# A two-block transformer kernel on one core: IN by quarters of K, modulation by 512 features and partly summed on VectorE, the second norm from columns

## The chip, the core and the metric

The kernel runs on one core of a Trainium2 chip. The metric is device time in microseconds of one execution (us).

## What is computed

Two transformer blocks follow each other on `x` (256 tokens, 2048 features, float32). The change touches the first alone:

```python
mod = silu(c) @ w_ada + b_ada                     # 2048 -> 6 * 2048
sh1, sc1, gt1, sh2, sc2, gt2 = split(mod, 6)
h = rmsnorm(x, g_norm_mix) * (1 + sc1) + sh1
proj = h @ w_in                                   # 2048 -> 3072: xr, gr, xp
xr = causal_dwconv(xr); hr = rg_lru(xr)
y = concat([hr * gelu(gr), pool_mixer(xp)]) @ w_out
x = x + gt1 * y
h = rmsnorm(x, g_norm_ffn) * (1 + sc2) + sh2
x = rmsnorm(x + gt2 * ((silu(h @ w_ffn_gate) * (h @ w_ffn_up)) @ w_ffn_down))
```

The second block (projection, retention, windowless block attention, merge, convolved FFN) is computed by code that the change leaves alone but for semaphore counts.

## The kernel before

Activations lie feature-major: 16 blocks of 128 features by 256 tokens. Each product runs in **slabs** of 256 output features and **chunks** of 512 rows of K (`KT` = 4 blocks of 128). A chunk's weights are 512 KB. Chunks are numbered through the program as G: IN has slabs 0 to 11 (G 0 to 47), OUT 12 to 19 (G 48 to 79), FFN1 starts at slab 20 (G 80) with gate and up slabs in turn.

Float32 values are multiplied as a high and a low part of type fp32r. Per chunk SP loads `raw` (a ring of 8), ACT copies the high part into `split` (a ring of 4, `convert` L793), DVE writes the low part (`convert` L1118), and PE multiplies each block of 128x128 twice (L512 and L514): high weights by the high and low activations side by side, 512 columns, and low weights by the high activations, 256 columns:

```python
pe.matmul(ps[:, s, b, :], split[:, slot, k, 0, ...], acts[:, k0 + k, :, :], ...)    # 512 columns
mm = pe.matmul(ps[:, s, b, 0:T], split[:, slot, k, 1, ...], acts[:, k0 + k, 0, :], ...)  # 256
```

A slab's product is then evicted: ACT copies the half with the low activations (`copy_low` L801, line L806), DVE adds the other (`evacuate` L1124, L1132). PE waits for the eviction of the slab before last.

**The modulation** is 12 parts of 1024 features; a part is 8 pieces of 1 MB (256 rows of K by 1024 columns). `multiply_ada` (L523, matmuls at L539) multiplies one piece by `c_act`, four products side by side in the array's columns; after the eighth ACT copies the row (`copy_row` L826, line L830), `turn_ada` (L543, matmuls at L547) turns it into a column and `finish_ada` (L1155, line L1158) adds the bias. Two parts (the scale and the shift of features 0 to 1023) come ahead of IN. The others **ride**: `RIDE_AT` (L95) names the chunk behind which a piece is multiplied, one a chunk in G 0 to 15, then four in five chunks. The pieces' loads stand in SP's one queue ahead of the weights of chunk G + 8, each waiting for its slot in a ring of 4, later of 2. Part 11 is stored in another order and read with a step of 8 (L537). Four pieces (`FILLERS`, L96) are multiplied while PE waits for the second norm.

**IN** runs its first eight slabs in two halves of K (`half_slab` L612): sixteen chunks over features 0 to 1023 of h, whose partial sums DVE keeps in `xr_pad` and `pool_x`, then sixteen over the rest, whose h is made at the border (L858 on ACT, L1202 on DVE). Convolution, gates, windows and recurrence follow in helpers called between chunks (`first_mid`, L924 on ACT and L1383 on DVE).

**The second norm** lies between OUT and FFN1: DVE sums the squares (L1173), PE spreads the sum over all partitions with a matrix of ones (`sum_squares` L559, L566 and L567), DVE, ACT and DVE form 1/rms over 256 columns (L1177, L854, L1188), then each block is scaled (L1197), shifted and rounded (L858), and its low part taken (L1202). FFN1's first slab waits for four blocks per chunk.

## Time and profile before

| | us |
|---|---|
| median of 3 runs (lowest, highest) | 2656.75 (2651.25, 2659.0) |
| the profiled execution, its own time | 2656.45 |
| its span | 2654.7 |
| TensorE busy | 2581.5 (97%) |
| VectorE busy | 1715.6 (65%) |
| ScalarE busy | 1183.7 (45%) |

Busy time is what an engine spent in instructions. The span runs from the first to the last instruction; the execution's own time lies 1.75 us above it. The mean granted TensorE clock is 0.986.

### The profile page before, as it was taken

The page shows a single profiled execution, that of the slowest core. Times are in us where ns is not written, and L with a number is a line of the kernel's source. Part 1 is how long each engine was busy: PE and PEld are TensorE (multiplying, and loading weights), DVE is VectorE, ACT ScalarE, POOL GpSimd, SP SyncE. Part 2 cuts the span into 40 slices and gives each one's busy share as a digit, 9 for nine tenths or more (in the row PEclk, how much of TensorE's full clock was granted, in tenths as well). Part 3 has the DMA queues.
Part 4 walks back from the last instruction along what each step waited for, and adds up shares of the span by engine and source line. Part 5 has one row for each costly group of instructions (what it writes and reads, how often), then busy time and mean ns, then how long its engine had stood idle before and what let it go on. Part 6 is the DMA issues. An engine that isn't in the chain of part 4 may idle for free.

```text
span 2654.7 us, 40107 instructions
## 1 busy us (share of the span) xinstructions
PE 2581.5 (97%) x14708; PEld 2140.2 (81%) x14708; DVE 1715.6 (65%) x2235; ACT 1183.7 (45%) x1441; POOL 9.9 (0%) x37
## 2 busy tenths in 40 slices
PE   4999998999999999999999999999999999999997
PEld 0667665788888888888888888888888888888886
DVE  2568445455555555577677565577788758875886
ACT  1345334344444444463444454455544444444443
POOL 1000000000000000000000000000000000000000
PEclk8999998999999999999999999999999999999998
DMA  9978988655555555565555555555555555565553
GB/s 374 400 272 328 348 328 296 211 190 190 190 190 189 191 189 189 164 190 179 178 172 172 167 163 188 189 184 189 174 190 189 183 185 183 185 192 181 189 171 114
DMA packets 155797, 553.91 MB, mean 209 GB/s; under 512 B 15648, under 2 KB 19744, under 8 KB 155696
## 3 DMA queue, kind: packets, MB, share of 16 engines
q1 hardware_dynamic: 154848, 549.84, 61.3%
q0 software_dynamic: 848, 2.69, 0.3%
q8 instruction: 67, 1.10, 0.2%
q14 instruction: 34, 0.28, 0.0%
HBM read 550.38 MB, written 2.10 MB: 208 GB/s over the span
## 4 chain that ended last, share of the span: by engine, by line
PE 92%; DMA 3%; DVE 2%; ACT 1%; issue 1%; SPq 0%; DVEq 0%; ACTq 0%
PE ps L512 55%; PE ps L514 28%; PE pm L539 3%; DMA ride<-in_w_ada 3%; PE ps L507 2%; PE ps L509 1%; DVE split L1121 1%; ACT split L799 0%; PE pm L547 0%; PE pm L684 0%; PE pm L608 0%; DVE x_t L1224 0%; DVE h_s L1423 0%; DVE val L1132 0%; ACT sq_gf L845 0%
## 5 line engine op out<-in xcount | busy, mean ns | idle before, releaser
L1121 DVE TENSOR_TENSOR split<-raw,split 128x1024 fp32r<-128x1024 f32 (+1 forms) x864 | 1032.5, 1203 | 808.2 <-ACT split L799 803.6
L799 ACT ACTIVATE split<-raw 128x1024 fp32r<-128x1024 f32 (+1 forms) x864 | 897.6, 1043 | 1211.5 <-PE ps L514 1154.1
L512 PE MATMUL ps<-h_s,split 128*128 128x512 f32 x3904 | 1383.5, 399 | 11.4 <-DVE split L1121 6.4
L514 PE MATMUL ps<-h_s,split 128*128 128x256 f32 x3904 | 1091.4, 280 | 0.0
L512 PEld LDWEIGHTS ps<-h_s,split 128*128 128x128 f32 x3904 | 735.0, 188 | 231.8 <-issue 54.5
L512 PE MATMUL ps<-mid_s,split 128*128 128x512 f32 x2368 | 833.3, 397 | 0.7 <-DVE split L1121 0.7
L514 PEld LDWEIGHTS ps<-h_s,split 128*128 128x128 f32 x3904 | 738.1, 189 | 0.5
L514 PE MATMUL ps<-mid_s,split 128*128 128x256 f32 x2368 | 661.7, 279 | 0.0
L512 PEld LDWEIGHTS ps<-mid_s,split 128*128 128x128 f32 x2368 | 444.3, 188 | 124.6 <-issue 17.3
L514 PEld LDWEIGHTS ps<-mid_s,split 128*128 128x128 f32 x2368 | 446.5, 189 | 0.0
L539 PE MATMUL pm<-ride,c_act 128*1 128x512 f32 x768 | 119.9, 703 | 39.0 <-DMA ride<-in_w_ada 39.0
L806 ACT ACTIVATE low<-ps 128x512 f32<-128x512 f32 x232 | 134.6, 580 | 4.4 <-PE ps L514 4.4
L507 PE MATMUL ps<-split,h_s 128*128 128x512 f32 x256 | 91.2, 401 | 0.0
L1132 DVE TENSOR_TENSOR val<-ps,low 128x512 f32<-128x512 f32 x128 | 87.4, 683 | 3.8 <-ACT low L806 3.7
L1503 DVE SCALAR_TENSOR_TENSOR conv_o<-up_pad,par,conv_o 128x256 f32<-128x256 f32 x176 | 77.5, 482 | 11.4 <-DVE conv_o L1501 5.6
L539 PEld LDWEIGHTS pm<-ride,c_act 128*1 128x1 f32 x768 | 10.6, 81 | 84.6 <-DMA ride<-in_w_ada 46.7
L509 PE MATMUL ps<-split,h_s 128*128 128x256 f32 x256 | 71.8, 280 | 0.0
L1134 DVE TENSOR_TENSOR low<-ps,low 128x512 f32<-128x512 f32 x88 | 60.1, 683 | 0.2
L507 PEld LDWEIGHTS ps<-split,h_s 128*128 128x128 f32 x256 | 48.1, 188 | 13.3 <-issue 1.7
L509 PEld LDWEIGHTS ps<-split,h_s 128*128 128x128 f32 x256 | 48.3, 189 | 0.0
L512 PE MATMUL ps<-o_r,split 128*128 128x512 f32 x128 | 45.5, 398 | 0.0
L512 PE MATMUL ps<-o_m,split 128*128 128x512 f32 x128 | 44.9, 393 | 0.0
(225 smaller groups left out, 1030.7 us busy)
## 6 DMA issues: line engine op xcount, KB each, us to landing
raw<-in_w_in SPq DMA_DIRECT2D x224, 512.0 KB, 3.4
ride<-in_w_ada SPq DMA_DIRECT2D x88, 1024.0 KB, 7.8
raw<-in_w_ffn_down SPq DMA_DIRECT2D x128, 512.0 KB, 3.9
raw<-in_w_ffn_gate SPq DMA_DIRECT2D x88, 512.0 KB, 3.5
raw<-in_w_ffn_up SPq DMA_DIRECT2D x88, 512.0 KB, 3.8
raw<-in_w_ffn_a SPq DMA_DIRECT2D x88, 512.0 KB, 3.9
raw<-in_w_ffn_b SPq DMA_DIRECT2D x88, 512.0 KB, 4.4
raw<-in_w_out SPq DMA_DIRECT2D x64, 512.0 KB, 5.1
```

Source lines behind the costliest of these rows:

```text
L507: pe.matmul(ps[:, s, b, :], acts[:, k0 + k, 0, b * P:(b + 1) * P], split[:, slot, k, :, :].rearrange("p h n -> p (h n)"), start=start, sto ...
L509: mm = pe.matmul(ps[:, s, b, 0:SLAB], acts[:, k0 + k, 1, b * P:(b + 1) * P], split[:, slot, k, 0, :], start=False, stop=stop)
L512: pe.matmul(ps[:, s, b, :], split[:, slot, k, 0, b * P:(b + 1) * P], acts[:, k0 + k, :, :].rearrange("p h t -> p (h t)"), start=start, sto ...
L514: mm = pe.matmul(ps[:, s, b, 0:T], split[:, slot, k, 1, b * P:(b + 1) * P], acts[:, k0 + k, 0, :], start=False, stop=stop)
L539: mm = pe.matmul(pm[2 + n % 2][g:g + 1, :], c_act[:, k:k + 1], moving, start=(i == 0), stop=(i == PIECES - 1))
L799: act.activation(split[:, c, 0:kt, 0, :], raw[:, CHUNKS * s + c, 0:kt, :], ACT.Copy).then_inc(hi_ready, 1)
L806: act.activation(low[:, s, :, :], ps[:, s, :, T:2 * T], ACT.Copy).then_inc(low_copied, 1)
L1121: dve.tensor_tensor(split[:, c, 0:kt, 1, :], raw[:, CHUNKS * s + c, 0:kt, :], split[:, c, 0:kt, 0, :].bitcast(F32), ALU.subtract).then_inc ...
L1132: ins = dve.tensor_tensor(dst, ps[:, s, :, 0:T], both, ALU.add)
L1134: own(dve.tensor_tensor(both, ps[:, s, :, 0:T], both, ALU.add))
L1503: ins = dve.scalar_tensor_tensor(out=dst, in0=src, scalar=w, in1=dst, op0=ALU.mult, op1=ALU.add)
```

## The change

1. **Groups of 512 features.** Scale and shift of the first norm (parts 0 to 3) become eight groups (`UNITS`) of four 1 MB pieces, each 512 rows of K by 512 columns. Only the first two groups stand ahead of IN; the others ride in G 0 to 20, eight pieces in five of each eight chunks. Five further parts ride from G 24, one piece a chunk in eight of nine chunks.
2. **IN in quarters of K.** The first eight slabs run in four passes of eight chunks (`one_chunk`). Each block is multiplied by three matmuls of 256 columns into one sum. ACT copies the sums of the first pass, DVE adds those of the others to them; ACT's `copy_low` isn't needed there. The h blocks of the next pass are made in chunks 3 to 6 of the pass before. The helpers between chunks get new places (`GATES_AT`, `WINDOWS_AT`, `POOL_AT`).
3. **Three parts are summed on DVE**: part 7 in OUT (G 60 to 75), parts 10 and 11 in FFN1 (G 88 to 119). A load of 128 rows (512 KB) is multiplied by `c_act` and added to a 128x1024 sum, and PE turns the sum with eight small matmuls (`turn_sums`). The fillers go.
4. **The second norm from columns.** PE takes the sum of squares as one column per 128 tokens, 1/rms is formed on 128x2, put on a diagonal and spread by two matmuls. ACT loads the table of the square root ahead of OUT. FFN1's first gate and up slabs take turns chunk by chunk, and the gate's wait for each block of h (`first_pair`).

The core of the diff:

```diff
-ADA_ORDER = (2, 0, 3, 1, 4, 5, 8, 6, 9, 7, 10, 11)
+LATE_PARTS = (4, 5, 8, 6, 9, 7, 10, 11)
+UNITS, UNIT_PIECES = 2 * CHUNKS, 4
+TENSOR_PARTS = 5
+OUT_ADDS = 1 * DB
+OUT_ADD_RING, FFN_ADD_RING = 6, 4
...
 def _rides():
-    at = list(range(HALF_CHUNKS))
-    at += [HALF_CHUNKS + r + r // 4 for r in range(6 * PIECES)]
-    at += [CHUNKS * 20 - 1] * (FILL_BEFORE + FILL_AFTER)
-    at += [CHUNKS * 20 + 2 + 2 * r for r in range(2 * PIECES - FILL_BEFORE - FILL_AFTER)]
+    at = [PASS_SLABS * p + c for p in range(CHUNKS - 1) for c in (0, 0, 1, 1, 2, 3, 3, 4)]
+    at += [PASSES - PASS_SLABS + r + r // 8 for r in range(TENSOR_PARTS * PIECES)]
     return at
...
+ADD_AT = [CHUNKS * 15 + j for j in range(OUT_ADDS)] + [CHUNKS * 22 + j for j in range(2 * DB)]
+GATES_AT = (26, 28, 30, 32)
+WINDOWS_AT = (32, 33, 37, 42)
+POOL_AT = (34, 36, 40, 44)
...
+        def load_add(j):
+            where, slot, _ = add_slot(j)
+            if j == 0:
+                sp.wait_ge(chunk_used, CHUNKS * S_OUT)
+            elif j == OUT_ADDS:
+                sp.wait_ge(ada_multiplied, UNITS * UNIT_PIECES + TENSOR_PARTS * PIECES)
+            if OUT_ADD_RING <= j < OUT_ADDS:
+                sp.wait_ge(ada_added, j - OUT_ADD_RING + 1)
+            elif j >= OUT_ADDS + FFN_ADD_RING:
+                sp.wait_ge(ada_added, j - FFN_ADD_RING + 1)
...
+            sp.dma_start(where, src).then_inc(add_loaded[slot], 16)
...
+        def turn_sums(g):
+
+            pe.wait_ge(ada_added, DB * (g - ADD_GROUPS + 1))
+            pe.wait_ge(mod_ready, g - 1)
+            sums = ada_sums(g)
+            for j in range(8):
+                block = sums[:, j * P:(j + 1) * P] if late_part(g) < ADA_FIRST else \
+                    sums.rearrange("q (p j) -> q j p", j=8)[:, j, :]
+                mm = pe.matmul(pm[2 + g % 2][:, j:j + 1], block, ones[:, 0:1], start=True, stop=True)
             mm.then_inc(ada_turned, 1)
...
+        def one_chunk(G):
+
+            c, q = divmod(G, PASS_SLABS)
+            if G >= 2:
+                pe.wait_ge(evacuated, G - 1)
+            if q == 0:
+                pe.wait_ge(h_ready, KT * (c + 1))
+            pe.wait_ge(lo_ready, G + 1)
+            for k in range(KT):
+                for b in range(2):
+                    weights = split[:, G % RING, k, :, b * P:(b + 1) * P]
+                    out, acts = ps[:, G % 2, b, 0:T], h_s[:, c * KT + k, :, :]
+                    pe.matmul(out, weights[:, 0, :], acts[:, 0, :], start=(k == 0), stop=False)
+                    pe.matmul(out, weights[:, 0, :], acts[:, 1, :], start=False, stop=False)
+                    mm = pe.matmul(out, weights[:, 1, :], acts[:, 0, :], start=False, stop=(k == KT - 1))
+            mm.then_inc(chunk_used, 1)
+            ride_along(G)
...
-        sum_squares(1)
-        for piece in FILLERS:
-            multiply_ada(piece)
-
+
+
+        pe.wait_ge(ssq_added, OUT_SLABS * 2)
+        for b in range(2):
+            for k in range(2):
+                mm = pe.matmul(pm[1][:, b:b + 1], ssq[:, k, b * P:(b + 1) * P], ones[:, 0:1], start=(k == 0), stop=(k == 1))
+        mm.then_inc(ssq_summed, 1)
+        pe.wait_ge(diag_ready, 1)
+        for b in range(2):
+            mm = pe.matmul(pm[1][:, T + b * P:T + (b + 1) * P], ones[:, :], diag[:, b, :], start=True, stop=True)
+        mm.then_inc(rstd_spread, 1)
+
+
+        def first_pair(gu):
+
+            for i in range(2 * CHUNKS):
+                G, s, c = CHUNKS * gu + i, i % 2, i // 2
+                if c == 0:
+                    pe.wait_ge(evacuated, evac_count_of(gu + s) - 1)
+                multiply(G, G % RING, s, h_s, c * KT, KT, c == 0, c == CHUNKS - 1,
+                         ready=DB + c * KT if s == 0 else None)
...
+            if c > 0:
+                dve.wait_ge(chunk_used, G + 1)
+                if G == PASS_SLABS:
+                    dve.wait_ge(evacuated, PASS_SLABS)
+                dve.tensor_tensor(pass_sum(q), ps[:, G % 2, :, 0:T], pass_sum(q), ALU.add).then_inc(evacuated, 1)
...
+            if c < CHUNKS - 1 and q == 6:
+                for b in range(first, first + KT):
+                    norm_low(0, 0, b)
```

**PE, the opening of IN.** Rows with `ride` and `ride_88` (or `ride_89`) are pieces of the modulation, `sel,row` the turns, `ps` the products of IN. Before, from the sum of squares on:

```order
L566 MATMUL pm<-ssq,ones 128x256
L567 MATMUL pm<-ssq,ones 128x256
L539 MATMUL pm<-ride,c_act 1x512 x4
L539 MATMUL pm<-ride_88,c_act 1x512 x8
L547 MATMUL pm<-sel,row 128x2 x4
L539 MATMUL pm<-ride,c_act 1x512 x8
L539 MATMUL pm<-ride_88,c_act 1x512 x8
L539 MATMUL pm<-ride,c_act 1x512 x8
L539 MATMUL pm<-ride_88,c_act 1x512 x8
L547 MATMUL pm<-sel,row 128x2 x4
L512 MATMUL ps<-h_s,split 128x512
L514 MATMUL ps<-h_s,split 128x256
```

Now, from the same instruction:

```order
L650 MATMUL pm<-ssq,ones 128x256
L651 MATMUL pm<-ssq,ones 128x256
L599 MATMUL pm<-ride_89,c_act 1x512 x4
L616 MATMUL pm<-sel,row 128x1 x4
L599 MATMUL pm<-ride,c_act 1x512 x8
L599 MATMUL pm<-ride_89,c_act 1x512 x8
L616 MATMUL pm<-sel,row 128x1 x4
L708 MATMUL ps<-h_s,split 128x256
L709 MATMUL ps<-h_s,split 128x256
L710 MATMUL ps<-h_s,split 128x256
```

IN's first matmul stands behind 32 matmuls of the modulation and not 64, and comes in threes.

**SP, from the first weights of IN.** Before:

```order
L384 DMA raw<-in_w_in 128x1024 x8
L396 DMA ride<-in_w_ada 128x2x1024
L384 DMA raw<-in_w_in 128x1024
L396 DMA ride<-in_w_ada 128x2x1024
L384 DMA raw<-in_w_in 128x1024
L396 DMA ride_88<-in_w_ada 128x2x1024
L384 DMA raw<-in_w_in 128x1024
```

The queue now:

```order
L422 DMA raw<-in_w_in 128x1024 x8
L437 DMA ride<-in_w_ada 128x4x512 x2
L422 DMA raw<-in_w_in 128x1024
L437 DMA ride_89<-in_w_ada 128x4x512 x2
L422 DMA raw<-in_w_in 128x1024
L437 DMA ride<-in_w_ada 128x4x512
L422 DMA raw<-in_w_in 128x1024
L437 DMA ride<-in_w_ada 128x4x512
L437 DMA ride_89<-in_w_ada 128x4x512
L422 DMA raw<-in_w_in 128x1024
L437 DMA ride_89<-in_w_ada 128x4x512
L422 DMA raw<-in_w_in 128x1024 x4
```

One piece and one chunk of weights took turns here; now the eight pieces of a group pair stand in front of five of eight chunks.

**SP, the loads for chunks 60 and on**, in OUT. `raw` is a chunk of weights, `add_out` a load for a sum on DVE. Before, in OUT:

```order
L384 DMA raw<-in_w_out 128x1024
L396 DMA ride<-in_w_ada 128x2x1024
L384 DMA raw<-in_w_out 128x1024
L396 DMA ride<-in_w_ada 128x2x1024
L384 DMA raw<-in_w_out 128x1024 x2
```

Now:

```order
L441 DMA ride<-in_w_ada 128x2x1024
L456 DMA add_out<-in_w_ada 128x1024
L422 DMA raw<-in_w_out 128x1024
L441 DMA ride<-in_w_ada 128x2x1024
L456 DMA add_out<-in_w_ada 128x1024
L422 DMA raw<-in_w_out 128x1024
```

The loads of the sums stand between the pieces and the weights, for eight chunks with both.

## Rows read from the trace of the kernel before

**Rows 1.** The page, part 1: busy us, share of the span, instructions.

```profile
PE 2581.5 (97%) x14708; PEld 2140.2 (81%) x14708; DVE 1715.6 (65%) x2235; ACT 1183.7 (45%) x1441; POOL 9.9 (0%) x37
```

**Rows 2.** The chain of waits in order of time: start, us, what.

```profile
59.19 1.93 PE pm L539 x8
...
69.72 0.77 PE ps L512
...
78.04 0.97 PE pm L539 x8
...
109.80 0.97 PE pm L539 x8
```

**Rows 3.** The instruction timeline of PE, the eighth piece: start, us, line, operation.

```profile
37.28 1.89 PE L539 MATMUL pm<-ride,c_act 128*1 128x512 f32 x8 [0.91 <-DMA ride<-in_w_ada]
```

**Rows 4.** Table of windows, 70 to 134 us; DMA packets of 3:13 and 19:31.

```profile
70.00:134.00 64.00, 64.00 (x383) 41.97 (x383) 31.12 (x39) 23.89 (x29) 0.00 (x0) 0.98 1.01 403
DMA packets 2489, 3.63 MB, mean 363 GB/s; under 512 B 52, under 2 KB 2100, under 8 KB 2489
DMA packets 1254, 4.86 MB, mean 405 GB/s; under 512 B 67, under 2 KB 67, under 8 KB 1254
```

**Rows 5.** Timeline, the end of one chunk with its ride, and the next.

```profile
130.00 0.40 PE L512 MATMUL ps<-h_s,split 128*128 128x512 f32 x1
...
130.23 0.28 PE L514 MATMUL ps<-h_s,split 128*128 128x256 f32 x1
...
130.44 1.04 PE L539 MATMUL pm<-ride,c_act 128*1 128x512 f32 x8
...
131.41 0.50 PE L512 MATMUL ps<-h_s,split 128*128 128x512 f32 x1
131.52 0.19 PEld L514 LDWEIGHTS ps<-h_s,split 128*128 128x128 f32 x1
```

**Rows 6.** Timeline, weight loads of a turn.

```profile
390.11 0.98 PEld L547 LDWEIGHTS pm<-sel,row 128*128 128x128 f32 x8
```

**Rows 7.** Timeline, the border between the halves of K.

```profile
134.44 1.04 PE L539 MATMUL pm<-ride,c_act 128*1 128x512 f32 x8
...
137.82 0.69 DVE L1132 TENSOR_TENSOR pool_x<-ps,low 128x512 f32<-128x512 f32 x1
...
138.54 3.26 DVE L1202 SCALAR_TENSOR_TENSOR h_s<-xc,mod,h_s 128x256 fp32r<-128x256 f32 x8
...
140.32 0.76 PE L512 MATMUL ps<-h_s,split 128*128 128x512 f32 x1 [3.06 <-issue]
...
145.06 1.04 PE L539 MATMUL pm<-ride,c_act 128*1 128x512 f32 x8
```

**Rows 8.** Timeline, a piece of part 11 in FFN1, and the next chunk.

```profile
452.49 2.01 PE L539 MATMUL pm<-ride,c_act 128*1 128x512 f32 x8
454.43 0.50 PE L512 MATMUL ps<-h_s,split 128*128 128x512 f32 x1
```

**Rows 9.** Timeline, the second norm and FFN1's first chunks.

```profile
404.98 1.22 PE L566 MATMUL pm<-ssq,ones 128*128 128x256 f32 x2 [3.54 <-DVE ssq L1173]
...
409.86 0.88 DVE L1197 SCALAR_TENSOR_TENSOR val<-x_t,gain,rstd 128x256 f32<-128x256 f32 x2
...
422.67 0.48 DVE L1202 SCALAR_TENSOR_TENSOR h_s<-val,mod,h_s 128x256 fp32r<-128x256 f32 x1 [0.18 <-ACT h_s L858]
...
419.77 0.80 PE L512 MATMUL ps<-h_s,split 128*128 128x512 f32 x1
...
430.28 1.04 PE L539 MATMUL pm<-ride,c_act 128*1 128x512 f32 x8
```

**Rows 10.** Waits of PE, 206 to 400 us: us, times, longest.

```profile
PE pm L539 <- DMA ride<-in_w_ada: 2.0, 4, 0.8
```

**Rows 11.** Windows, 514 to 600 us (PE, PEld, DVE, ACT); a DVE group of the page by shapes.

```profile
514.00:600.00 86.00, 86.00 (x498) 75.23 (x497) 49.65 (x50) 38.38 (x43) 0.00 (x0) 1.00 0.58 189
L1327 DVE SCALAR_TENSOR_TENSOR lru_t<-a_sq,lru_t 128x1024 f32<-128x1024 f32 x2 | 2.5, 1226 | 0.1
```

More of the change, by code:

```diff
@@ L499, in slab, with multiply @@
                     after(c)
-        def multiply(G, slot, s, acts, k0, kt, first, last, tok=False):
+        def multiply(G, slot, s, acts, k0, kt, first, last, tok=False, ready=None):
             pe.wait_ge(lo_ready, G + 1)
             for k in range(kt):
+                if ready is not None:
+                    pe.wait_ge(h_ready, ready + k + 1)
                 start, stop = first and k == 0, last and k == kt - 1
@@ L960, in pool_high @@
             ins.then_inc(pool_hi, 1)
[L962 to L966 removed]
+        for G in range(PASSES):
+            ahead = G + RING
+            convert(ahead // (2 * CHUNKS), ahead // CHUNKS % 2, ahead % CHUNKS)
+            if G < PASS_SLABS:
+                act.wait_ge(chunk_used, G + 1)
+                act.activation(pass_sum(G), ps[:, G % 2, :, 0:T], ACT.Copy).then_inc(evacuated, 1)
+            first_mid(G)
+            if G % PASS_SLABS == 6 and G < PASSES - PASS_SLABS:
+                first = KT * (G // PASS_SLABS + 1)
+                act.wait_ge(mod_ready, first // 2 + 2)
+                for b in range(first, first + KT):
+                    norm_block(0, 0, b)
+        for q in range(PASS_SLABS, IN_SLABS):
+            turn(q // 2, q % 2, mid=lambda c: first_mid(CHUNKS * q + c))
         gelu(3)
         y_high(3)
+        act.activation(s_inv[:, :], inv_n[:, 0:2], ACT.Sqrt)
         for q in range(OUT_SLABS):
@@ new lines, in finish_rides @@
+        def finish_rides(G):
+            for g, at in LAST_RIDE.items():
+                if at + 1 == G:
+                    finish_ada(g)
+            for j, at in enumerate(ADD_AT):
+                if at == G:
+                    k, sums = j % DB, ada_sums(ADD_GROUPS + j // DB)
+                    piece, slot, times = add_slot(j)
+                    dve.wait_ge(add_loaded[slot], 16 * times)
+                    if k == 0:
+                        dve.tensor_scalar(sums, piece, c_act[:, k:k + 1], None, ALU.mult).then_inc(ada_added, 1)
+                    else:
+                        dve.wait_ge(ada_added, j)
+                        dve.scalar_tensor_tensor(out=sums, in0=piece, scalar=c_act[:, k:k + 1], in1=sums,
+                                                 op0=ALU.mult, op1=ALU.add).then_inc(ada_added, 1)
+            for g, at in LAST_ADD.items():
+                if at + 3 == G:
+                    a = late_part(g) * 8
+                    dve.wait_ge(ada_turned, g + 1)
+                    dve.tensor_tensor(mod[:, a:a + 8], pm[2 + g % 2][:, 0:8], col("b_ada", a, 8), ALU.add).then_inc(mod_ready, 1)
@@ L1416, in _ @@
+        for q in range(PASS_SLABS, IN_SLABS):
+            turn(q // 2, q % 2, val[:, q % 2, :, :], mid=lambda c: first_mid(CHUNKS * q + c))
         gated(3)
```

532 lines of the change are left out of this document (272 added, 260 removed).

## The prediction

> **What bounds the kernel now.** I read the page first: TensorE is busy for 97% of the span [rows 1]. So time is won where it idles or does work that can go elsewhere; the modulation and its waits lie ahead of about 510 us. The chain of waits, read in order of time, gives the opening: sixteen 1 MB modulation pieces land one by one, the last is multiplied at 59.19, and the first matmul of IN starts at 69.72 [rows 2]. The eighth piece was multiplied at 37.28 [rows 3]. The table of windows says what holds this stage: the DMA engines are full (403 GB/s in the first 16 chunks) while TensorE never pauses [rows 4]. The instruction timeline gives prices: a chunk with its ride goes from 130.44 to 134.44; over the eight from 78.04 to 109.80 in the chain it is 3.97 us [rows 2, 5]. A chunk alone is 8 pairs of matmuls, 498 matmuls in 86.00 us, so 0.345 a pair and 2.77 a chunk [rows 11]. A ride thus costs 1.19, of which 0.97 is its own (130.44 to 131.41 [rows 5]) and 0.22 the change-over. Two holes are left: the second half of K, no matmul of IN from 135.4 to 140.32 [rows 7], and the second norm, where FFN1 starts at 419.77 [rows 9].
>
> The sum is made against the profiled execution's 2656.45 us (span 2654.7), 0.3 below the median of the runs. A difference under 0.3% (8 us) can't be told from none.
>
> **The change, part by part.**
>
> *Start: -20.7.* Only two groups of four pieces precede IN. They use the same ring, so the eighth comes where it did, and the path behind the last piece keeps its length (59.19 to 69.72 is 10.53: turn, gain, four blocks of norm, first conversion). That moves the start by 59.19 - 37.28 = 21.9. But the pieces now come in rows of 2 KB. Of the trace's packets, 2489 of 1.46 KB on average took 10 us of 16 engines, 64 ns each, and 1254 of 3.9 KB took 12 us, 153 ns each [rows 4]. Between them 2 KB costs about 86 ns, so a piece (512 packets, 16 engines) takes 2.7 us, not 2.55, and eight pieces 1.2 us more. IN starts near 49.
>
> By the Trainium skill ("DMA: Bandwidth & Descriptors", the overview table) anything from 512 B up runs at line rate, so this 1.2 us and the first pass's share of as much would not exist, and the time would be 2617. The rows above differ, and I go by them.
>
> *First pass: +2.2.* By SP's order, shown with the change, eight raw chunks (4.2 MB, 10.2 us at 410 GB/s) go ahead of the third group's pieces. With piece 8 of the run landing near 51.4 and a piece or chunk behind it every 2.7 or 1.27 us, the rides at chunks 1 and 3 wait about 1 us each for their second piece, and the pass ends near 86. From then on a pass moves 12.6 MB in 32 us and TensorE needs 34, so no wait is left.
>
> *Borders of K: -1.2.* The border before costs 4.9 idle (135.41 to 140.32) and 1.8 at the low clock (that chunk took 4.74, not 2.97), 6.7 in all [rows 7]. Now there are three. At each, ACT and DVE first convert, DVE adds the pass sum (0.69), and then four low parts at 0.41 (eight took 3.26 [rows 7]): ready 4.9 behind chunk 6's end, where chunk 7 covers 2.8. That is 2.1 twice, and 1.3 in the first pass (its sum is on ACT): 5.5.
>
> *Rides: -21.7.* Before, 96 pieces: 16 in the opening, 6 in the norm's hole, 74 on the path at 1.19, and part 11's eight, read with a stride, take 0.97 more each (452.49 to 454.43 [rows 8]): 88.1 + 7.8 = 95.9. Now 64: three passes with eight pieces in five chunks (8 x 0.97 + 5 x 0.22 = 8.9) and forty singles, 26.6 + 47.6 = 74.2.
>
> *Turns: +9.4.* A turn is 8 records in 0.98, 0.93 on the path [rows 6]. Nine become eleven (8.3 to 10.2), and three sums of 16 records come in, 1.9 each, the last by eight-strided weights, which I double as the pieces' stride does [rows 8]: 7.5. Left alone it would be 1.9 less.
>
> *Three matmuls for two: -2.4.* In eight slabs a pair of 512 and 256 columns becomes three of 256. The 512 starts 0.23 before the 256, the next comes 0.12 behind it [rows 5]. Three at 0.112 are 0.336 for 0.345, times 256. The doubt is the weight load, which lasts 0.19 and now has only short matmuls above it. The row of turns answers: eight loads of 128x128 back to back in 0.98, one in 0.11 [rows 6]. If loads didn't overlap it would be 3 x 0.19, +56 in all: the upper bound, far from that row.
>
> By the Trainium skill ("TensorE: Matmul & The Clock Gate", Back-to-back issue gap) a matmul costs N/2.4 + 2.5 ns, so a third one would only add a floor, +0.6. The trace's 512-column start distance of 0.23 is longer than that, which is where my gain comes from.
>
> *Second norm: -8.0.* Ahead of it little changes: TensorE's sums over 256 columns (from 404.98), and the statistics and reciprocal over 256 columns until the first scaled block at 409.86 [rows 9] become eight records of one column (about 1.9 at the low clock), small instructions and one spread, from which I get 409.2. The gain is behind: the first pair takes h block by block. Blocks come every 0.79 (409.86 to 422.67 for 16), TensorE starts at the first, near 411.3, does chunks 80 to 83 (11.1, and 2.3 for the low clock, as 419.77 to 430.28 is 10.5 for 3 x 2.77 and the change-over) and is through at 424.4, just as ACT and DVE deliver chunk 84. Before it would be there at 432.9, rides apart. Half a us goes back at chunk 88, which waits for the gate's eviction one chunk earlier.
>
> *Sums in OUT and FFN1: +5.* 48 DVE instructions of 128x1024, 1.23 each [rows 11]. In FFN1 a pair of slabs has 22.2 us; DVE is busy 49.65 of 86, 12.9 a pair, and eight sums make it 22.7. That is as much as there is, but conversions run four chunks ahead (6 us in hand), so four such pairs cost nothing; without this cover they cost 2 to 6. What does cost is OUT: chunks 60 to 67 have ride, sum and weights, 2.1 MB or 5.1 us at 410 GB/s, against 3.97. Eight times 1.14 is 9.1, the upper bound; zero is the lower, if queued loads run ahead. Chunk 59 has no ride, so the queue begins some 4 us ahead: I take 5. Rides waited 2.0 in four places before [rows 10], and I leave that as it is. SP's other loads keep eight chunks of lead. The weights' reordering in FFN1's first pair, the longer unrolled part and the removed evictions on ACT lie under TensorE's work: 0.
>
> Sum: -20.7 + 2.2 - 1.2 - 21.7 + 9.4 - 2.4 - 8.0 + 5 = -37.4, so **2619**.
>
> **The rivals.**
> 1. *DVE or ACT binds*, in slabs 8 to 11 (decays in two adjacent chunks, four windows, both multipliers, with about 2 us in hand by my count) and in FFN1. For: 22.7 against 22.2. Against: DVE is busy for 65% over the span, and the ring of four is deep. Price 4 and 6: 2629.
> 2. *DMA binds more than I take*: OUT's full 9.1, the passes another 4, and a wait behind every eighth ride: 2629. For: 403 GB/s in the stage at issue [rows 4]. Against: the 16-chunk stage there ran on without a pause.
> 3. *A third matmul gains nothing*: if each short one starts 0.12 behind the last, as the 512 does behind the 256, three take 0.36 against 0.345, +3.8 and not -2.4: 2625. For: 0.12 is read at 0.01 [rows 5]. Against: the turns' 0.11 [rows 6]. The floor of the Trainium skill's page on TensorE points the same way.
> 4. *The early start is swallowed*: the change doesn't do what it says, since the bytes of IN bind and TensorE waits out what it won, 2640. Against: until pass 3 ends some 67 MB move, 166 us at 403 GB/s, and TensorE isn't there before about 190.
> 5. *Slower: weight loads bind.* In IN's eight slabs no long matmul covers two loads. It decides once a load's distance passes 0.19 us, and three at 0.19 make 0.56: 2619 + 2.4 + 56 = 2677. Rows 6 speak against it.
>
> **How the numbers follow.** Forecast 0.55, rival 1 0.14, rival 2 0.12, rival 3 0.06, rival 4 0.06, rival 5 0.04, the rest 0.03 for something unforeseen. The low end takes OUT's 5 and the first pass's 2.2 as nothing, an unhurt strided turn and a border or two that close: 2608. The high end adds rival 1's 10, two borders with the low clock (1.8 each) and 4 of OUT's bound: 2637. Outside are rivals 4 and 5 and a tail. Faster by over 0.3% is every case but rival 5 and part of the rest: 0.94, same 0.01, slower 0.05.
>
> **What would show it.** First IN matmul near 49 (start); rides waiting for DMA in chunks 0 to 4 alone (first pass); idle of 1 to 2 us ahead of chunks 8, 16 and 24 at the full clock (borders); a chunk of 24 matmuls in 2.7 us (three for two; 4.5 would be rival 5); FFN1's first matmul near the first block of h and some 13 us later the fifth chunk (norm); waits on ride pieces in chunks 60 to 67 of 5 in sum (OUT), and none on split in FFN1. The prediction is wrong if TensorE waits for split, for the pass sums or for `mod` anywhere ahead of 480 us, or if the time behind FFN1's second group differs from before.

## The result

| | us |
|---|---|
| before, median of 6 runs (lowest, highest) | 2657.34 (2651.25, 2659.45) |
| the change, median of 6 runs (lowest, highest) | 2635.09 (2630.65, 2646.09) |
| ratio of the two, 95% interval | 0.9926 [0.991, 0.9941] |
| predicted | 2619.0 (2608 to 2637) |
| the change's profiled execution (span) | 2646.09 (2644.3) |

The change gains about 20 us (0.74%, between 16 and 24 us by the interval). The direction is right and the median lies in the range, but the forecast was 37: about half of it came. The profiled execution is the slowest of its six.

### The profile page after: what moved, and what is told of

The parts are those of the page before. It is cut to its first block, busy times and chain, and to the rows that moved or that the text cites. A ratio compares the mean times of both kernels' runs of the same rounds, so it can differ in the third digit from the quotient of the medians.

```text
span 2644.3 us, 40425 instructions
## 1 busy us (share of the span) xinstructions
PE 2567.1 (97%) x14836; PEld 2170.0 (82%) x14836; DVE 1771.2 (67%) x2291; ACT 1182.5 (45%) x1436; POOL 9.9 (0%) x37
## 4 chain that ended last, share of the span: by engine, by line
PE 90%; DMA 4%; DVE 3%; ACT 1%; issue 1%; SPq 0%; DVEq 0%; ACTq 0%
PE ps L576 53%; PE ps L578 27%; DMA ride<-in_w_ada 4%; PE ps L571 2%; PE ps L573 1%; PE ps L708 1%; PE pm L599 1%; DVE split L1225 1%; PE ps L710 1%; PE ps L709 1%; PE pm L606 1%; ACT split L907 1%; PE pm L792 0%; DVE xc L1406 0%; DVE val L1318 0%
## 5 line engine op out<-in xcount | busy, mean ns | idle before, releaser
L576 PE MATMUL ps<-h_s,split 128*128 128x512 f32 x3648 | 1295.7, 400 | 4.1 <-DVE h_s L1323 1.7
L578 PE MATMUL ps<-h_s,split 128*128 128x256 f32 x3648 | 1023.9, 281 | 0.0
L576 PEld LDWEIGHTS ps<-h_s,split 128*128 128x128 f32 x3648 | 687.2, 188 | 186.4 <-issue 16.3
L578 PEld LDWEIGHTS ps<-h_s,split 128*128 128x128 f32 x3648 | 690.6, 189 | 0.4
L913 ACT ACTIVATE low<-ps 128x512 f32<-128x512 f32 x216 | 125.2, 579 | 4.4 <-PE ps L578 4.4
L708 PE MATMUL ps<-h_s,split 128*128 128x256 f32 x256 | 76.6, 299 | 11.2 <-DVE split L1225 6.1
L709 PE MATMUL ps<-h_s,split 128*128 128x256 f32 x256 | 73.5, 287 | 0.0
L710 PE MATMUL ps<-h_s,split 128*128 128x256 f32 x256 | 73.4, 287 | 0.0
L708 PEld LDWEIGHTS ps<-h_s,split 128*128 128x128 f32 x256 | 50.0, 195 | 25.7 <-issue 24.8
L599 PE MATMUL pm<-ride,c_act 128*1 128x512 f32 x256 | 37.2, 681 | 26.0 <-DMA ride<-in_w_ada 26.0
L571 PEld LDWEIGHTS ps<-split,h_s 128*128 128x128 f32 x256 | 48.1, 188 | 13.3 <-issue 1.7
```

The lines of the kernel that those rows point to most:

```text
L571: pe.matmul(ps[:, s, b, :], acts[:, k0 + k, 0, b * P:(b + 1) * P], split[:, slot, k, :, :].rearrange("p h n -> p (h n)"), start=start, sto ...
L576: pe.matmul(ps[:, s, b, :], split[:, slot, k, 0, b * P:(b + 1) * P], acts[:, k0 + k, :, :].rearrange("p h t -> p (h t)"), start=start, sto ...
L578: mm = pe.matmul(ps[:, s, b, 0:T], split[:, slot, k, 1, b * P:(b + 1) * P], acts[:, k0 + k, 0, :], start=False, stop=stop)
L708: pe.matmul(out, weights[:, 0, :], acts[:, 0, :], start=(k == 0), stop=False)
L709: pe.matmul(out, weights[:, 0, :], acts[:, 1, :], start=False, stop=False)
L710: mm = pe.matmul(out, weights[:, 1, :], acts[:, 0, :], start=False, stop=(k == KT - 1))
```

## The profile after

Part 1 of the page (busy time, its share, instructions), against [rows 1]:

```profile
PE 2567.1 (97%) x14836; PEld 2170.0 (82%) x14836; DVE 1771.2 (67%) x2291; ACT 1182.5 (45%) x1436; POOL 9.9 (0%) x37
```

DVE took on 56 us of work and ends at 67%.

The instruction timeline of PE at the start (start, duration, engine, line, operation; in brackets the idle time before it and what ended it), against [rows 2, 3]:

```profile
37.91 1.04 PE L599 MATMUL pm<-ride,c_act 128*1 128x512 f32 x8 [0.54 <-DMA ride<-in_w_ada]
39.66 1.05 PE L616 MATMUL pm<-sel,row 128*128 128x1 f32 x8 [0.71 <-ACT row L937]
46.84 0.55 PE L708 MATMUL ps<-h_s,split 128*128 128x256 f32 x1 [6.13 <-DVE split L1225]
...
53.56 1.04 PE L599 MATMUL pm<-ride,c_act 128*1 128x512 f32 x8 [1.13 <-DMA ride<-in_w_ada]
...
61.56 1.04 PE L599 MATMUL pm<-ride,c_act 128*1 128x512 f32 x8 [1.66 <-DMA ride<-in_w_ada]
```

The eighth piece is multiplied 0.63 later than before, IN starts 22.9 earlier, and then the second piece of each early pair of rides is waited for. Windows of PE from 20 to 34 us, while the pieces land, before and now (window: length, PE busy, matmuls, granted clock, DMA share, GB/s):

```profile
20.00:34.00 14.00, 9.46 (x52) 1.00 1.03 411
```

```profile
20.00:34.00 14.00, 10.50 (x52) 0.97 1.05 387
```

The DMA engines are fully busy in both, and move 387 GB/s in rows of 2 KB for 411 in rows of 4 KB.

PE's longest waits from 40 to 530 us (what waited, for what: us in total, times, longest):

```profile
PE pm L606 <- DMA ride<-in_w_ada: 8.1, 10, 1.5
...
PE pm L737 <- DVE ssq L1294: 5.7, 1, 5.7
PE ps L708 <- issue: 5.1, 3, 2.0
PE pm L599 <- DMA ride<-in_w_ada: 4.9, 4, 1.7
PE ps L576 <- DVE h_s L1323: 1.7, 1, 1.7
PE pm L741 <- DVE diag L1595: 1.3, 1, 1.3
PE pm L692 <- DVE mid_s L1469: 1.2, 1, 1.2
```

The first row is single rides (6.5 of it in chunks 60 to 67; for before see [rows 10]), the third the three borders of K ([rows 7]), the fourth the first pass. At the second border the granted clock fell in this execution:

```profile
120.00:130.00 10.00, 8.05 (x56) 0.83 0.65 245
```

Chunk 16 took 4.2 us from 123.81, where its work at the full clock is 2.9; with its two rides it was 6.4 us, where it took 4.9 in again, whose clock stayed at 1.00 there behind the same idle time.

The second norm, against [rows 9], PE's timeline first and DVE's behind it:

```profile
401.86 1.86 PE L737 MATMUL pm<-ones,ssq 128*128 128x1 f32 x8 [5.66 <-DVE ssq L1294]
405.00 1.23 PE L741 MATMUL pm<-diag,ones 128*128 128x128 f32 x4 [1.28 <-DVE diag L1595]
407.95 0.77 PE L576 MATMUL ps<-h_s,split 128*128 128x512 f32 x1 [1.73 <-DVE h_s L1323]
```

```profile
403.83 0.16 DVE L1591 TENSOR_SCALAR s_sum<-pm 128x2 f32<-128x2 f32 x1 [1.94 <-PE pm L737]
406.26 0.87 DVE L1318 SCALAR_TENSOR_TENSOR val<-x_t,gain,pm 128x256 f32<-128x256 f32 x2 [1.32 <-PE pm L741]
```

FFN1 starts 1.7 us behind the first scaled block; before it was 9.9 (409.86 to 419.77). The turns of the last two sums, plain and with the step of 8:

```profile
483.16 1.84 PE L629 MATMUL pm<-ones,acc_ffn 128*128 128x1 f32 x16
...
529.33 3.85 PE L629 MATMUL pm<-ones,acc_ffn 128*128 128x1 f32 x16
```

**Where the time went.** The starts of chunks in the two timelines give this table. The middle column is the prediction's terms, sorted by stretch:

| chunks | before, us | after, us | predicted difference | measured |
|---|---|---|---|---|
| to the first of IN | 69.7 | 46.8 | -20.7 | -22.9 |
| 0 to 32 | 142.3 | 151.6 | -0.2 | +9.3 |
| 32 to 60 | 113.9 | 122.7 | +5.3 | +8.8 |
| 60 to 80 | 93.8 | 86.7 | -6.8 | -7.1 |
| 80 to 88 | 29.8 | 25.2 | -5.5 | -4.6 |
| 88 to 104 | 61.0 | 44.5 | -16.0 | -16.5 |
| 104 to 124 | 55.5 | 63.6 | +5.7 | +8.1 |
| to chunk 124 | 566.1 | 541.2 | -38.2 | -24.9 |
| from there to the end of the span | 2088.6 | 2103.1 | 0 | +14.5 |

(-38.2 and not -37.4: the kernel before has ten turns in this stretch, the prediction counted nine.) The last row was forecast as nothing. It falls into 10.4 us in FFN1 and 4.1 at the program's end, and both look the same in windows of PE, of before and of the change:

```profile
600.00:700.00 100.00, 100.00 (x579) 1.00 0.59 189
2450.00:2550.00 100.00, 100.00 (x579) 1.00 0.56 185
```

```profile
600.00:700.00 100.00, 100.00 (x567) 1.00 0.56 185
2450.00:2550.00 100.00, 100.00 (x568) 1.00 0.52 173
```

The same pairs of matmuls, TensorE never idle, the granted clock 1.00, and yet 567 matmuls fall in 100 us where 579 did: a pair starts every 0.353 us, not every 0.3467. I call them the slow and the quick pace.

## Experiments

Two theories. **A**: the missing gain lies in terms of the sum ahead of chunk 124 (three matmuls for two, waits for DMA), and the pace behind it is drawn anew in each execution. **B**: the change, its last turn above all, brings the slow pace into FFN1.

### The change again, and the kernel before again

The first four are the change unaltered, the fifth the kernel before.

> The changed kernel, unaltered. In the profile of the change the pairs of matmuls in FFN1 started every 0.353 us (567 matmuls in 100 us at a granted clock of 1.00), in the kernel before every 0.3465 us (579), which cost about 13 us between 530 and 1150 us. Theory A (the pace is drawn anew in each execution and has nothing to do with the change): this execution's FFN1 may stand at either pace, and where it stands at 579 its own time is 2630 to 2634 us. Theory B (the change causes the slow pace in FFN1, by the strided turn of the last sum or by the added loads and sums): FFN1 stands at 567 again, own time 2640 to 2646 us.

> The changed kernel for a third profile. Theory B says FFN1 stands at 567 in about one of two (three of seven profiles so far with the strided last turn, none of seven without it); theory A gives the same chance to every kernel. The end of the program (from 2313 us in the time of the kernel before) stands at 567 again if it belongs to the program.

> The changed kernel for a fourth profile. As for the third: by theory B FFN1 stands at 567 in about one of two, and the end of the program at 567 if that belongs to the program.

> The changed kernel beside it: median 2634 to 2638 if the two differ as they did so far; 2628 or less if the difference was one of chips. Fifth profile of its FFN1: 567 or 579 matmuls in 100 us, about as likely (two of four so far).

> The kernel before, unaltered, to see whether the pace of a pair of matmuls is drawn anew here too. In its profile FFN1 (from 533 us) started 579 matmuls in 100 us, the second FFN (2000 to 2300 us) 567. If it is drawn in each execution, one of the two may come out the other way this time, and the granted clock there stays 1.00. If it belongs to the stage and the program, both come out as before.

Measured: again 2636.7 us (2627.25 to 2639.1), again_2 2633.67, again_3 2641.89, again_4 2640.7 (2632.33 to 2647.81). With the first six runs, the change has 20 runs with a median of 2636.8. PE in the windows of again and again_3 (again_4 has 569 in FFN1):

```profile
600.00:700.00 100.00, 100.00 (x578) 1.00 0.58 190
```

```profile
600.00:700.00 100.00, 100.00 (x567) 1.00 0.55 186
2450.00:2550.00 100.00, 100.00 (x579) 1.00 0.53 178
```

FFN1 is quick in again and again_2, slow in again_3 and again_4: one and the same program has both. Laid over each other from chunk 130 on, the profiles differ in three stretches alone: FFN1 (+10.4 us at the slow pace, three of the change's five profiles), the second FFN's middle (-3 to -8 where a part of it is quick) and the last 300 us (+3 to +4). Everything else agrees to 0.3 us, but for about 1 us in the last 60. before_again took 2656.14, with FFN1 at 578, the second FFN at 567 and the end at 579 in 100 us, all as in the first profile of that kernel. In again_3 the end was quick too, so that pace isn't the program's own either.

Ahead of chunk 130 two more things differ between these five profiles. The low clock behind a border of K came at chunk 16 in four of them (6.3 us to the next chunk, 4.9 without it) and at chunk 24 in two (5.5 for 4.0). And the slow pace shows in chunks 88 to 104 too, ahead of the last turn, here in the change and in again:

```profile
440.00:470.00 30.00, 30.00 (x175) 1.00 0.91 334
```

```profile
440.00:470.00 30.00, 30.00 (x172) 1.00 0.89 322
```

The change is quick there and slow in FFN1 behind it, again the other way round. Of all twenty profiles sixteen are slow in this stretch (a pair every 0.353 us), those of the kernel before and of six of the seven kernels with a plain last turn among them.

### The last turn

plain_turn and plain_turn_2, from the change:

```diff
-                block = sums[:, j * P:(j + 1) * P] if late_part(g) < ADA_FIRST else \
-                    sums.rearrange("q (p j) -> q j p", j=8)[:, j, :]
+                block = sums[:, j * P:(j + 1) * P]
...
-        a["w_ada"][0][:, ADA_FIRST * ADA_COLS:].reshape(D, len(RIDE_PARTS), ADA_COLS // P, P).transpose(0, 1, 3, 2)
-    ).reshape(D, len(RIDE_PARTS), ADA_COLS)
+        a["w_ada"][0][:, ADA_FIRST * ADA_COLS:]).reshape(D, len(RIDE_PARTS), ADA_COLS)
```

> Part 11 is stored as the other parts are, so the last sum is turned without the step of 8. In the profile of the change the strided turn took 3.71 us against 1.70 for the plain ones. Both theories: the turn takes 1.7 us, 2.0 less. Theory A: nothing else changes, the median is 2 us below the unaltered kernel's. Theory B with the strided turn as cause: FFN1 behind chunk 121 keeps 579 matmuls in 100 us in every profile, and the median is 10 us or more lower.

> The kernel with the plain last turn once more, unaltered. Its first four runs lay between 2630.5 and 2635.5, while the runs of the change went from 2627 to 2646. Theory B: again all within 6 us and FFN1 at 579 matmuls in 100 us. Theory A: one run in three comes out 10 us higher, with FFN1 or the end of the program at 567.

three_turns, from the plain turn:

```diff
-            for j in range(8):
+            for j in list(range(8)) * (3 if g == GROUPS - 1 else 1):
```

> The last sum is turned without the step of 8, but three times over (48 matmuls of one column, 5.1 us, in place of 16 strided ones in 3.7). If the stretch without full matmuls is what lets the granted clock fall behind the strided turn, it falls here too (about 0.7 over 10 us), and FFN1 may then stand at either pace. If it is the strided read, the clock stays at 1.00 and FFN1 at 579.

holes_step8 is the kernel holes (below) with the step of 8 kept:

> The kernel with rides in the holes, but with the last sum turned with the step of 8 as in the change. In the six profiles with this turn at that place TensorE's granted clock fell behind it in five (0.66 to 0.83 over the 10 us from 530), in the two with the plain turn never, and the slow pace of FFN1 (567 matmuls in 100 us) came in two of the six. Theory A (pace drawn by chance alone): the median is 2 to 4 us above the kernel with holes, and its runs lie within 6 us of each other as that kernel's. Theory B (the strided turn opens the way to the slow pace in some executions): of six runs one or more lies 10 us or more above the lower half, and the profile may show 567.

Measured: plain_turn 2632.91 us (2630.54 to 2635.5), plain_turn_2 2628.45 (2624.63 to 2631.45, none 10 us higher), eight runs with a median of 2631.0: 5.8 below the change (3.8 in the four runs beside again). Theory B had asked for 10 or more, theory A for 2. holes_step8 2626.11 (2620.45 to 2635.79), 0.3 above holes in the median; its profiled run, with FFN1 at 568, is the 2635.79; three_turns 2632.36 in one run. The turn in the timelines of plain_turn and three_turns:

```profile
528.83 1.84 PE L628 MATMUL pm<-ones,acc_ffn 128*128 128x1 f32 x16
```

```profile
527.44 5.42 PE L628 MATMUL pm<-ones,acc_ffn 128*128 128x1 f32 x48
```

PE's windows behind it, in plain_turn, three_turns and the change (FFN1 at 578 and 579 in 100 us in the first two):

```profile
530.00:540.00 10.00, 10.00 (x62) 1.00 0.53 160
```

```profile
530.00:540.00 10.00, 10.00 (x59) 0.83 0.32 105
```

```profile
530.00:540.00 10.00, 10.00 (x40) 0.66 0.32 107
```

The plain turn takes 1.84 for 3.85, and the clock behind it stays at 1.00. Chunks 104 to 124 take 59.2 us, not 63.6 (again 62.8): 3.6 to 4.4 less, of which 2.0 is the turn and 1.6 to 2.4 the low clock behind it. With 48 plain matmuls of one column, 5.4 us of them, the clock falls too, so the step isn't needed for it. Behind the strided turn it fell in nine of ten profiles. As for FFN1's pace: in ten profiles of kernels with the step of 8 at the last turn it was slow five times (the change, row_norm, holes_step8, again_3, again_4), in ten without such a turn never (both of before, before_unrolled and the seven with a plain last turn). If the turn made no difference, so uneven a split of the five would come in about one case in 60; against the seven plain turns alone, which differ from the change in less, in one of 25. And the theory was made after the first of the five had been seen. So the count favours B and does not prove it, and the pace itself needs no strided turn: chunks 88 to 104 are slow in kernels of every kind. How a turn opens the way to the slow pace isn't shown: in one_sum_load the strided turn left the clock at 1.00 and FFN1 was quick, in again, wide_again, slab_by_slab and three_turns the clock fell and FFN1 was quick too.

### Six pairs written out in the kernel before

```diff
-RIDE_SLABS = (LAST_RIDE[ADA_PARTS - 1] + 3) // CHUNKS + 1
+RIDE_SLABS = (LAST_RIDE[ADA_PARTS - 1] + 3) // CHUNKS + 1 + 4
```

> The kernel before with six pairs of FFN1's slabs written out and not four, as in the change; nothing else differs. Behind FFN1 all twelve profiles of changed kernels lose 4 us against both profiles of the kernel before, between 2313 and 2600 us: there the kernel before starts 579 matmuls in 100 us, the others 567. If the length of the written-out program sets this pace: this kernel stands at 567 there and takes 4 to 5 us more than the kernel before. If the pace is drawn, or comes from another part of the change: 579 here, and no difference.

Measured: 2656.42 us (10 runs), ratio 0.9994 [0.9982, 1.0005]. Its window at the end:

```profile
2450.00:2550.00 100.00, 100.00 (x568) 1.00 0.54 181
```

The end of this profile is slow, its median no longer. Together with again_3's quick end: this pace comes and goes in both programs. The end was slow in 16 of 17 profiles of changed kernels, and in one of three of the kernel before (this one). So the changed kernels may meet it more often, which three profiles can't settle; the longer program costs nothing in the medians.

### Three matmuls for two

```diff
-                    pe.matmul(out, weights[:, 0, :], acts[:, 0, :], start=(k == 0), stop=False)
-                    pe.matmul(out, weights[:, 0, :], acts[:, 1, :], start=False, stop=False)
+                    pe.matmul(ps[:, G % 2, b, :], weights[:, 0, :], acts.rearrange("p h t -> p (h t)"), start=(k == 0), stop=False)
```

> The four passes of IN use the old pair (512 and 256 columns) in place of three matmuls of 256; the sum of high weights by low activations is then left out of these slabs' result, nothing else. In the profile of the change each of the three starts 0.119 to 0.120 us behind the last, a block of 128x128 takes 0.357 to 0.360, and the pair takes 0.3465. Theory A (three short matmuls cost more than the pair, the third rival of the prediction): IN's 256 blocks take 2.7 to 3.5 us less, the first matmul behind the fourth pass comes that much earlier. Theory C (the prediction's own term: three are as cheap as 0.336): 2.4 us more.

Measured: 2633.11 us (2624.9 to 2644.74). PE's timeline in again and in wide_again:

```profile
99.89 0.28 PE L708 MATMUL ps<-h_s,split 128*128 128x256 f32 x1
100.01 0.28 PE L709 MATMUL ps<-h_s,split 128*128 128x256 f32 x1
...
100.25 0.28 PE L708 MATMUL ps<-h_s,split 128*128 128x256 f32 x1
```

```profile
99.78 0.40 PE L708 MATMUL ps<-h_s,split 128*128 128x512 f32 x1
100.01 0.28 PE L709 MATMUL ps<-h_s,split 128*128 128x256 f32 x1
100.13 0.40 PE L708 MATMUL ps<-h_s,split 128*128 128x512 f32 x1
```

Three take 0.36, two take 0.35. A chunk without rides and away from the borders (chunks 6, 14 and 22) lasts 2.95 to 2.96 us with three, in every profile, and 2.86 with the pair. The whole stretch, chunks 0 to 32, lasts 149.0 us with the pair; with three, rides in their places, it lasts 150.9 on average over eleven profiles, but between 148.0 and 152.2, by the waits of the first pass and the low clock at the borders. So the sign is theory A's, shown by the chunks; the size is not settled by one profile with the pair, and 0.09 in each of 32 chunks, 2.9 us, is the most. The prediction's own term (2.4 the other way) falls.

### The sums in OUT

```diff
         if j < OUT_ADDS:
-            slot = j % OUT_ADD_RING
-            return add_out[:, slot, :], slot, j // OUT_ADD_RING + 1
+            return add_out[:, 0, :], 0, 1
...
         def load_add(j):
+            if 0 < j < OUT_ADDS:
+                return
```

> In OUT the sixteen DVE sums all read the first loaded slot, so fifteen loads of 512 KB are not issued; part 7 of the modulation is then wrong, all other work is done. In the profile of the change the rides in chunks 60 to 67 waited 6.5 us in sum for their pieces, where before they waited about 2.0. If the DMA engines' rate is the cause: these waits go (at most 1 us left in sum), the second norm begins 5 to 6 us earlier. If the DVE sums are the cause (DVE late with conversions, so loads late): the waits stay near 6 us.

Measured: 2630.44 us (2622.27 to 2643.39). PE's waits from 320 to 400 us, in the change and here:

```profile
PE pm L606 <- DMA ride<-in_w_ada: 6.5, 6, 1.5
```

```profile
PE pm L607 <- DMA ride<-in_w_ada: 1.3, 3, 0.7
```

Fifteen loads of 512 KB less take the waits from 6.5 to 1.3, while DVE does the same sums. Chunks 60 to 88 take 106.5 us, not 111.9 (111.5 in again): the loads were the cause and not the sums, and the term is 5.

### The second norm

slab_by_slab:

```diff
-                if i == 0:
-                    s, c = G % 2, (G - CHUNKS * S_FFN) // 2
...
-                G, s, c = CHUNKS * gu + i, i % 2, i // 2
+                G, s, c = CHUNKS * gu + i, i // CHUNKS, i % CHUNKS
```

> FFN1's first gate slab runs whole before its first up slab, still waiting block by block. In the profile of the change the first pair took 25.18 us from its first matmul to chunk 88. The prediction's term (its gain of 8 us lies behind the norm, in the chunks taking turns): the first four chunks would follow the blocks of h, sixteen every 0.79 us, so 12.6 us for 11.1 of work, then 11.1 for the up slab: 23.7 at the full clock and up to 2.3 more for the low clock. So the turn-taking is worth 0 to 2 us of the stage, and the rest of the gain is the earlier first matmul (one block of h waited for, not four). Rival (the turn-taking carries the gain): the stage takes 29 us or more.

row_norm:

```diff
-        for b in range(2):
-            for k in range(2):
-                mm = pe.matmul(pm[1][:, b:b + 1], ssq[:, k, b * P:(b + 1) * P], ones[:, 0:1], start=(k == 0), stop=(k == 1))
...
+        sum_squares(1)
...
+        inv_rms(1)
```

> The second norm's 1/rms is made over 256 columns as in the kernel before; FFN1's first pair stays as changed. In the profile of the change it took 6.1 us from the first matmul of the column sums (401.86) to FFN1's first matmul (407.95). The prediction's term: the columns save 0.7 us ahead of the first scaled block. With rows I expect 1 to 2 us later. Rival (the columns save 3 us or more, since two instructions over 256 columns and a square root of them go): FFN1's first matmul 3 us or more later behind the sums.

Measured: slab_by_slab 2635.34 us (2631.7 to 2635.97), its stage 25.4 us from FFN1's first matmul to chunk 88 for 25.2 in the change. row_norm 2638.87 (2629.97 to 2646.38), with these rows:

```profile
399.76 1.22 PE L650 MATMUL pm<-ssq,ones 128*128 128x256 f32 x2 [5.66 <-DVE ssq L1285]
...
406.33 0.77 PE L576 MATMUL ps<-h_s,split 128*128 128x512 f32 x1 [4.50 <-DVE h_s L1314]
```

From the first matmul of the sums to FFN1 it is 6.6 with rows, 6.1 with columns. So the columns are worth 0.5 (1 to 2 had been expected), the turn-taking 0.2, and neither carries the gain.

### Rides in the holes, and two more moves

holes, on top of the plain turn:

```diff
-    at = [PASS_SLABS * p + c for p in range(CHUNKS - 1) for c in (0, 0, 1, 1, 2, 3, 3, 4)]
-    at += [PASSES - PASS_SLABS + r + r // 8 for r in range(TENSOR_PARTS * PIECES)]
+    at = [0, 0, 1, 1, 2, 3, 3, 4]
+    at += [PASS_SLABS * p + c for p in (1, 2) for c in (-1, -1, 0, 1, 2, 3, 3, 4)]
+    at += [23, *range(23, 30)] + [31 + r + r // 8 for r in range((TENSOR_PARTS - 1) * PIECES)]
```

> Beside the plain last turn, the rides are moved: two pieces each are multiplied ahead of chunks 8, 16 and 24, where TensorE idled 1.22, 1.95 and 1.95 us in the profile of the change, and the single rides end at chunk 65, not 67. Theory A (the holes at the borders come from ACT and DVE making the next blocks of h, TensorE has nothing else to do in them): two pieces (about 2.1 us with the change-over) fit into each hole, and the waits for pieces in chunks 60 to 67 get shorter by a quarter; chunk 80 starts 5 to 7 us earlier against the unaltered profile of the change, the median is 6 to 8 us below the unaltered one with the plain turn's 2 in it. Rival (the DMA engines, 94% busy in the first 200 us, bind the passes): the pieces moved forward are waited for, and the holes only change their name; 0 to 2 us beside the plain turn's.

spread and spread_2, on top of holes:

```diff
-ADD_AT = [CHUNKS * 15 + j for j in range(OUT_ADDS)]
+ADD_AT = [CHUNKS * 13 + 3 * j // 2 for j in range(OUT_ADDS)]
```

> As the kernel with rides in the holes, and OUT's sixteen sums start at chunk 52 and come two in three chunks, not one a chunk from chunk 60. Without fifteen of the sums' loads the stage from chunk 60 to 88 took 106.5 us against 111.5 and 111.9, and the waits for pieces fell by 5; in the kernel with holes, waits of 1.06, 2.40 and 0.77 for pieces were left in chunks 61 to 65. If it is the peak of the transfers there (ride, sum and weights in one chunk, 2.1 MB): the waits are cut to 1 or 2 us, chunk 80 starts 2 to 4 us earlier. If the whole of OUT is at the DMA engines' limit (94% busy from 300 to 400 us): the waits only move to chunks 52 to 60 and chunk 80 starts where it did.

> The best kernel so far (plain last turn, rides in the holes, OUT's sums spread) once more, beside the change on the same chip. Its first four runs had a median of 2623.5, the change's fourteen one of 2635.9: 12 us or 0.5% apart. If that holds, it lies at 2623 to 2626 here, with FFN1 at 579 matmuls in 100 us.

early_pieces, on top of spread:

```diff
         for G in range(RAW):
+            if G in (4, 6):
+                load_ada(2 * UNIT_PIECES + G - 4)
+                load_ada(2 * UNIT_PIECES + G - 3)
```

> As the kernel with spread sums, and the four pieces behind chunks 0 and 1 are loaded in front of raw chunks 4 and 6, not behind raw chunk 7. In the profiles of the change the pieces of the first pass were waited for 4.4 to 5.3 us. If only their place in the queue is the cause (eight raw chunks, 4.2 MB or 10 us, ahead of them): 3 to 4 us of these waits go, chunk 8 starts that much earlier. If the DMA engines' rate binds the pass (94% busy in the first 200 us): the waits go to later pieces or to the conversion, and chunk 8 starts at most 1 us earlier.

Measured: holes 2625.77 us (2621.23 to 2626.73), ratio to before 0.9873 [0.9859, 0.9888]; spread 2623.5 (2620.93 to 2627.87); spread_2 2618.7 (2616.07 to 2627.46; 2623 to 2626 had been expected), ratio 0.9862 [0.984, 0.9884], beside again_4's 2640.7 with 0.9941 [0.9918, 0.9964] on the same chip: the best version, ahead of both kernels; early_pieces 2626.54 (2625.05 to 2629.01). PE's waits from 60 to 200 us in again and in holes:

```profile
PE ps L708 <- issue: 5.1, 3, 2.0
PE pm L599 <- DMA ride<-in_w_ada: 1.7, 1, 1.7
```

```profile
PE pm L600 <- DMA ride<-in_w_ada: 1.7, 1, 1.7
PE pm L607 <- DMA ride<-in_w_ada: 1.6, 2, 0.8
```

The borders' 5.1 are gone, for 1.6 of new waits. Chunk 80 starts at 402.5, against 406.5 and 406.9 with the plain turn alone, 408.0 in the change and 409.8 in again: theory A of its expectation.

Spreading OUT's sums is the second case of its expectation: from 280 to 400 us the waits were these in holes and in spread, and chunk 80 started at 402.5 and 401.3 (402.8 in spread_2), too little to tell apart.

```profile
PE pm L607 <- DMA ride<-in_w_ada: 6.2, 8, 2.4
```

```profile
PE pm L607 <- DMA ride<-in_w_ada: 6.7, 8, 1.1
```

early_pieces gave one wait where spread had three, from 40 to 100 us (spread first):

```profile
PE pm L600 <- DMA ride<-in_w_ada: 3.5, 3, 1.7
```

```profile
PE pm L603 <- DMA ride<-in_w_ada: 3.4, 1, 3.4
```

The sum stayed, and the chunk behind the first border started at 90.80, not 89.41. The DMA engines are fully busy from 47 to 88 us in both (a share of 1.04, at 393 and 396 GB/s): the first pass is bound by their rate, and the order in the queue only chooses who waits.

## Why only half of the forecast gain came

Two steps of the prediction failed. In the stretch that it summed, its terms for chunks 0 to 32 came out 9.5 us too low: three matmuls for two had the wrong sign (-2.4 forecast, some 2 us more measured), the waits of the first pass were 4.9 and not 2.2, and the low clock at the borders was not in the sum. And everything behind chunk 124 was put at nothing, where the profiled execution took 14.5 us more at the slow pace. Averaged over the five profiles of the change and the three of the kernel before (before_unrolled among them), chunk 124 starts 23 us earlier (38 forecast) and the stretch behind it takes 5 more (0 forecast). That the median still lies in the range is luck: the upper end was made of rival 1's 10 us, which did not come.

By its own steps, against the table of stretches:

- **Start** (-20.7): measured -22.9. The 2 KB rows cost what the packet rows gave: 387 GB/s for 411, 5% a piece or about 1 us in eight. (By the Trainium skill, "DMA: Bandwidth & Descriptors", Specifications, they would cost nothing; the trace disagrees.) From the first to the eighth piece it was 18.9 us, and 17.9 to 18.2 in the three profiles of the kernel before. The path behind the last piece took 8.9, not the 10.5 that I carried over, and that was luck: it took 8.9 in before_unrolled too, and 10.6 in three_turns.
- **First pass** (+2.2): 4.9 in four waits. Mis-sized: I gave the queue one wait each in two chunks and no more. early_pieces shows that DMA's rate was the limit.
- **Borders of K** (-1.2): the idle time was 5.1 for 5.5 forecast. Left out was the low clock, some 1.5 at chunk 16 with its rides; I had it for the kernel before, and for this one in the high end of the range alone.
- **Rides** (-21.7): the counts hold (80 pieces before, 64 after), and so do the stretches 60 to 104 that rest on them (-28.3 forecast with the norm, -28.2 measured).
- **Turns** (+9.4): the doubled strided turn was right (3.7); the low clock behind it, 1.6 to 2.4, was not in the sum, nor was the tenth turn of before.
- **Three for two** (-2.4): this step failed by its sign. The short matmuls start 0.120 apart, not the 0.112 that I took from the eight weight loads of a turn, whose matmuls have two columns [rows 6]; the row of 256 columns behind 512 [rows 5] already showed 0.12, and rival 3 had read it. Removing them was worth 0.09 a chunk and 1.9 in the stretch on average, so forecast and measured are some 4 apart. By the Trainium skill's formula for a single matmul ("TensorE: Matmul & The Clock Gate", Back-to-back issue gap) an estimate for 256 columns is 109 ns; the trace has 120, and the measurement decides.
- **Second norm** (-8.0): from the last matmul of OUT to chunk 88 the kernel before took 45.5 us without its three rides and turn there (20.2 and 25.3), the change 37.0: -8.5. The size is right, the reason only in part. Turn-taking and columns give 0.7 together. What is left is that FFN1 starts at the first block. Before, the four filling rides held it, each waiting for its piece, as the timeline of the kernel before has it up to FFN1's start at 419.77 [rows 9]:

```profile
407.23 1.88 PE L539 MATMUL pm<-ride,c_act 128*1 128x512 f32 x8 [0.17 <-DMA ride<-in_w_ada]
...
414.14 1.89 PE L539 MATMUL pm<-ride,c_act 128*1 128x512 f32 x8 [1.46 <-DMA ride<-in_w_ada]
417.95 1.89 PE L539 MATMUL pm<-ride,c_act 128*1 128x512 f32 x8 [1.93 <-DMA ride<-in_w_ada]
```

  The fourth block's low part was done at 413.77 in DVE's timeline, 6.0 us earlier. Starting at the first block and not the fourth is worth three blocks at 0.79, 2.4 more. With the 0.5 of the columns this makes 8.9, where FFN1 started 8.7 sooner behind the first matmul of the sums (6.1 us for 14.8). This is read from rows; no run tested it alone.
- **Sums** (+5): 5.0 to 5.4 by one_sum_load; chunks 88 to 104 with sums on DVE take 44.5 us, which is 16 chunks without any wait at the quick pace (45.3 at the slow one in again): 0, as forecast. Rival 1 did not come.
- **Not in the sum**: in chunks 32 to 60 3.3 us of small waits (1.6 for pieces at chunks 40 to 50, 1.2 for the pool's low part, and the gates), and everything behind chunk 124, 14.5 us in the profiled execution.

Together: the terms ahead of chunk 124 missed 13.3 in this profile (9.5 of it in chunks 0 to 32: 2.7 in the first pass, some 4 in three for two, about 1 at the borders), and the pace behind it took 14.5 more there. The forecast's last sentence named the test by which it is wrong, a different time behind FFN1's second group, and that is so. What stays open: what makes the pace, why FFN1 was slow only behind the strided turn, and about 2 us of chunks 0 to 32.

## What to carry to other kernels

A hole in which an engine waits for another engine's work is the place for work that must be done anyway: moving six pieces of the modulation into three such holes brought chunk 80 forward by 4 us, while reordering loads in a stage that is short of DMA rate gave nothing. Price a new shape of instruction from the row of the nearest size, not from the smallest one. And a stretch of small matmuls can cost more than its own time: look at the granted clock behind it. Last, a stage of which every execution has its own pace is compared over several profiles, not over one pair.

## What the runs showed of the hardware

The same pair of matmuls (512 and 256 columns) on a TensorE that never idles at a granted clock of 1.00 has two paces, 579 and 567 matmuls in 100 us (distances 0.232 and 0.115, or 0.236 and 0.1175 us). A pace can hold for hundreds of microseconds (FFN1, chunk 124 to 1150 us), can change from one stage to the next, and differs between executions of one program. It moves this kernel by 10 us in FFN1, 3 to 4 at the end and up to 8 in the second FFN, and that is most of what its five profiled executions (2630.5 to 2646.1) differ by.
